# Rows of the activation buffers: A from 512 to 528 elements, B from 576 to 560

## The reference

```
# block 1: T = 256 tokens
a = rms_norm(x);  z = a @ w_in                  # 2048 x 5120: q, k, v, u, g
o = diff_attention(q, k, v) | spatial_gate(gelu(u), gelu(g))
h = x + o @ w_out                               # 2048 x 2048
f = rms_norm(h); h += (silu(f @ w1) * (f @ w3)) @ w2       # hidden 5632
h += (p @ pl_w_up) * sigmoid(h @ pl_w_gate);  x = rms_norm(h)
# block 2: T = 16 learned tokens + 256
hn = rms_norm(h); proj = hn @ w_in_2            # 2048 x 12288
y = g_a * pooled(u) @ pool_w * scale + g_b * ((gb * conv3(gc * v)) @ conv_out_w)
h += y @ w_o;  h += (silu(.) * .) @ w_down      # hidden 5632
out = rms_norm(h)[:, 16:]
```

## Time and profile before

| | |
|---|---|
| time, median of 3 runs | 2670.52 us (2670.02 to 2670.8) |
| span of the profiled execution | 2668.2 us |
| that execution's own time beside its span | not listed; the median is 2.3 us longer than the span |
| TensorE matmul busy | 2657.2 us, 15711 matmuls |
| TensorE weight load busy | 2349.5 us |
| VectorE busy | 1658.2 us |
| ScalarE busy | 1235.8 us |
| HBM read | 498.37 MB, 188 GB/s over the span |

### The profile page before, as it was taken

How to read it: one execution, slowest core, us unless ns; L and a number is a source line. 1 busy time by engine, 2 the same in 40 slices (tenths; PEclk the granted TensorE clock), 3 DMA queues, 4 the chain that set the end, 5 groups by cost and what they waited for, 6 DMA issues and landing times.

```text
span 2668.2 us, 39872 instructions
## 1 busy us (share of the span) xinstructions
PE 2657.2 (100%) x15711; PEld 2349.5 (88%) x15711; DVE 1658.2 (62%) x1645; ACT 1235.8 (46%) x1355; POOL 0.8 (0%) x7
## 2 busy tenths in 40 slices
PE   9999999999999999999999999999999999999998
PEld 7889888888888888888999999888888888888887
DVE  6567766555655556796676666556765645564555
ACT  5446554444444444565443333444554434443444
POOL 0000000000000000000000000000000000000000
PEclk9999999999999999999999999999999999999999
DMA  8554555556555555555555555555565555555554
GB/s 291 183 174 144 192 187 189 191 189 191 192 191 191 191 191 188 175 197 198 176 183 178 179 184 190 189 189 189 189 205 189 189 190 189 189 195 195 178 190 140
DMA packets 254251, 502.92 MB, mean 188 GB/s; under 512 B 8130, under 2 KB 11652, under 8 KB 253988
## 3 DMA queue, kind: packets, MB, share of 16 engines
q1 hardware_dynamic: 252180, 497.61, 56.5%
q10 hardware_dynamic: 1952, 3.68, 0.4%
HBM read 498.37 MB, written 2.88 MB: 188 GB/s over the span
## 4 chain that ended last, share of the span: by engine, by line
PE 99%; DVE 0%; ACT 0%; DMA 0%; issue 0%; ACTq 0%; DVEq 0%
PE ps L1356 49%; PE ps L1370 24%; PE ps L1389 4%; PE ps L1390 4%; PE ps L1391 4%; PE ps L1407 4%; PE ps L1408 4%; PE ps L1409 4%; PE ps L1399 0%; PE ps L1401 0%; PE ps L1400 0%; PE ps L1319 0%; DMA xtok<-in_x_dram 0%; PE ps L1543 0%; PE ps L1542 0%; PE ps L1544 0%
## 5 line engine op out<-in xcount | busy, mean ns | idle before, releaser
L822 DVE TENSOR_TENSOR lo<-raw,hi 128x1024 fp32r<-128x1024 f32 x940 | 1127.6, 1223 | 856.5 <-ACT hi L488 847.6
L488 ACT ACTIVATE hi<-raw 128x1024 fp32r<-128x1024 f32 x940 | 971.3, 1055 | 1065.3 <-PE ps L1370 479.0
L1356 PE MATMUL ps<-A,hi 128*128 128x512 f32 x3648 | 859.9, 392 | 0.0
L1356 PEld LDWEIGHTS ps<-A,hi 128*128 128x128 f32 x3648 | 675.1, 188 | 138.9
L1356 PE MATMUL ps<-B,hi 128*128 128x512 f32 x1984 | 481.7, 395 | 0.0
L1370 PEld LDWEIGHTS ps<-A,lo 128*128 128x128 f32 x3648 | 442.6, 188 | 11.5 <-DVE lo L822 0.2
L1370 PE MATMUL ps<-A,lo 128*128 128x256 f32 x3648 | 445.4, 278 | 0.0
L1356 PEld LDWEIGHTS ps<-B,hi 128*128 128x128 f32 x1984 | 364.4, 188 | 79.3
L1370 PEld LDWEIGHTS ps<-B,lo 128*128 128x128 f32 x1984 | 243.0, 188 | 10.3
L1370 PE MATMUL ps<-B,lo 128*128 128x256 f32 x1984 | 244.5, 277 | 0.0
L1408 PE MATMUL ps<-B,hi 128*128 128x258 f32 (+1 forms) x768 | 219.8, 286 | 0.0
(11 more groups left out here) (240 smaller groups left out, 1341.1 us busy)
## 6 DMA issues: line engine op xcount, KB each, us to landing
raw<-in_w_in_dram SPq DMA_DIRECT2D x136, 1024.0 KB, 5.1
raw<-in_ffn_w_dram SPq DMA_DIRECT2D x132, 1024.0 KB, 5.1
raw<-in_w_gate_up_dram SPq DMA_DIRECT2D x88, 1024.0 KB, 5.0
raw<-in_w_down_dram SPq DMA_DIRECT2D x44, 1024.0 KB, 5.1
raw<-in_w_out_dram SPq DMA_DIRECT2D x16, 1024.0 KB, 5.1
raw<-in_pl_w_gate_dram SPq DMA_DIRECT2D x16, 1024.0 KB, 5.1
raw<-in_conv_out_w_dram SPq DMA_DIRECT2D x16, 1024.0 KB, 5.1
raw<-in_w_o_dram SPq DMA_DIRECT2D x16, 1024.0 KB, 5.1
```

The source lines that it names most:

```text
L488: act.activation(hi[:, slot % RING], raw[:, raw_slot, 2 * (slot % 2):2 * (slot % 2) + 2, :], ACT.Copy).then_inc(hi_ready, 1)
L822: dve.tensor_tensor(lo[:, slot % RING], raw[:, slot // 2 % RAWS, 2 * (slot % 2):2 * (slot % 2) + 2, :], hi[:, slot % RING], ALU.subtract). ...
L1356: last = pe.matmul(ps[:, b0 + m, :], high(slot, kk, m), both, start=j == 0 and kk == 0, stop=ends and j == seg.pieces - 1 and kk == 1)
```

## The change

Rows of A are 528 elements long (2112 bytes) in place of 512 (2048), and those of B 560 (2240) in place of 576 (2304). Nothing is written to or read from the added elements. No instruction, loop or wait is touched; only the addresses are.

```
-BROW = 576
+BROW = 560
+AROW = 528
...
-        A = sb("A", [P, KT, 2 * T], F32R)
+        A = sb("A", [P, KT, AROW], F32R)
```

## The result

The changed kernel takes 2690.91 us (median of 4 runs, 2690.61 to 2691.1) against 2670.44 us before: +20.5 us, ratio 1.0077 with a 95% interval of [1.0065, 1.0089]. It is slower, by 0.8%.

A forecast was written before the change was run, and what follows sets the result against it. TensorE's start-to-start matmul pace was taken to bound the kernel, set by operand distance; terms of +7.8, -4.3, 0, +3.3, +2.3, -0.8 and 0 us gave +8.3, so 2678.8 us, with a range of 2650 to 2697.

The forecast's parts named there:

- rival (c): All rows: new distances as dear as 192 (2693 us), or each change of distance costs a step (+15 us); chance 0.16.
- the forecast's own span: Whole kernel: 2672 to 2686 us if a mix of distances sets the pace; chance 0.36.
- Distance with a period of 256: Moving operand's start less stationary's, modulo 256, sets the pace: 64 cheap, about 228.8 ns; 192 dear, about 233.2.
- The unknown distances: Half the rows, at distances 0 and 128: taken at the mean of cheap and dear, 231 ns for 512 columns.
- high on A: 3648 matmuls of high weights on A: 228.8 to 230.95 ns, +7.8 us.
- low on A: 3648 matmuls of low weights on A: left at 115.45 ns, 0 us.
- low on B: 1984 matmuls of low weights on B: 113.8 to 115.45 ns, +3.3 us.
- the sum of the ends: All terms with the unknown half of the rows at its bounds: -96 us (2574) to +65 us (2735).
- The mix of distances: Rows of A and B taking four distances: each kind's pace is the mean of its parts, no cost of changing.
- by token, B stationary: 1056 matmuls in the segments by token with B stationary: 228.9 to 231.1 ns, +2.3 us.
- A stationary: 384 matmuls in the segments by token with A stationary: 233.3 to 231.1 ns, -0.8 us.
- Wide: 2304 matmuls of 272 and 258 columns on B: 0 us, with bounds of -16 to +11 us.

The follow-up runs named there:

- e1: Kernel before, with vec2 (384 bytes) moved ahead of B so that B has A's distance of 64 from the weights: 2668.2 us, ratio 0.9992.
- e4: Kernel before, with small tensors reordered so that A starts 192 bytes past the weights as B_halves does: 2674.73 us, ratio 1.0017.
- e5: Kernel before, with only the weights (raw, hi, lo) moved by 64 bytes, A and B keeping their addresses: 2686.9 us, ratio 1.0063.
- e7: Kernel before, with only B's rows changed, to 544 elements, so they take distances 192 and 64 in turn: 2673.29 us, ratio 1.0012.
- e11: e9 with segments plgate, ga, gbr, cout and wo added to SNAKED, giving blocks of 32 there: 2671.01 us, ratio 1.0002 against the kernel before.
- e3: Kernel before, with small tensors reordered so that all rows of A and B_halves start 128 bytes past the weights: 2703.66 us, ratio 1.0125.
- e12: Kernel before at its own addresses, with segments plgate, ga, gbr, cout and wo added to SNAKED: 2681.53 us, ratio 1.0044.
- e9: Kernel before, rows unchanged, with A and B_halves 64 bytes past hi and lo 128 bytes further than hi: 2666.71 us, ratio 0.9987.
- e8: Kernel before, rows unchanged, with A and B_halves at distance 0 from hi and lo 64 bytes further than hi: 2669.55 us, ratio 0.9998.
- e2: Kernel before, with small tensors reordered so that A and B_halves both start 0 bytes past the weights: 2676.61 us, ratio 1.0024.

## Why the prediction was right, and where its sum was short

**Direction and range.** Slower, and 2690.9 lies within 2650 to 2697. It lies there because the range had been drawn out to rival (c); the forecast's own span, 2672 to 2686, misses it. The sum took +8.3 us where +20.5 came. The time is nearer to (c)'s 2693, to which I gave 0.16, and (c)'s two mechanisms, dear new distances and a cost of changing, are in part what happened. The direction was no luck: it came from high weights on A, the largest group, leaving a cheap distance, and that term held.

**What bounds the kernel.** Right. No engine and no DMA took part; the +20.8 us of span are steps from matmul to matmul. The strides for VectorE cost nothing (1226 ns for four rows of B before and after).

**Distance with a period of 256.** Right, and shown: e1 and e4 exchange the paces of A and B, and e5 moves them by moving the weights. The period shows after the change as well. In plgate and cout, rows k = 0 to 3 of A take 229.4, 233.8, 233.2 and 230.6 ns for high weights, and rows 4 to 7 take 229.6, 234.2, 233.3 and 230.6, 256 bytes further within 512 (means from the start times). What the prediction didn't have is that distance isn't all: the order and length of the blocks, and the order of the rows, choose among several paces of one distance (e7 to e11). The rule of the Trainium skill ("SBUF — State Buffer", section "Who interferes with whom": two independent read ports, and TensorE never waits on anyone) would have left the time at 2670.5. Measurements decide against it as a statement of pace: 64 bytes on the weights alone cost 16.7 us in e5. Where in the chip the steps are lost no run shows.

**The unknown distances, taken at the mean of the known.** For high weights that was nearly right: 227.8 at 0 and 233.0 at 128, mean 230.4, against my 231. The term "high on A" was +7.8 us and came out at +8.7. For low weights it was wrong: 119.7 and 118.6, against my 115.45. That is the term "low on A: I leave it there, 0" (came out +5.3) and "low on B, +3.3" (+8.0). I had the bound for them at 122.5, and no reason for the middle but that the paces seen were close to one another. The 115.45 wasn't even the middle of what had been seen: it is A's mean, and with B's 113.8 for distance 192 the same rule gives 114.6, that is -3.0 and +1.6 us in place of 0 and +3.3, and a sum further off. (In the sum of the ends, low on B is -5 and +10 us by the values given, not -7 and +11.)

**The mix of distances.** The forecast held that a mix costs the mean of its parts; I had put the cost of changing into (c), as 4.7 ns at each change, +15 us. From the steady table and the changed kernel: on A 231.4 - 230.8 = 0.6 ns a high matmul (+2.3 us) and 117.4 - 117.0 = 0.4 a low one (+1.5); on B 1.4 (+2.8) and 1.0 (+2.1); by token, B stationary, 232.2 against a mean of 230.4 (226.7, 233.3, 232.7 and 228.9 with B at 0, 64, 128 and 192), +1.8 ns (+1.8 us). Together some 10 to 11 us, half of the result, or about 3.2 ns for each of the 3248 changes. e7 shows such an excess by itself, with two distances. That it is paid for each change isn't shown: for low weights it can as well be the dearer of the paces that one distance allows, since with 117.8 for distance 64 the mean of the four is 117.4, what the changed kernel has on A. I dismissed a cost of changing because B's rows jumped by 256 bytes without a trace; that is no jump in distance at all, by the period that I had chosen myself.

**Token and wide segments.** By token, B stationary: +2.3 forecast, +3.3 measured for the 1008; the mean of the four steady paces would have made it +1.5. A stationary -0.8, measured -0.7. Wide 0, measured -2.4 us, within its bounds. (Of the 258-column ones, those of lines 1407 and 1409 start 56 bytes into the row, at 184 modulo 256 and not at 128.)

**What the profile after was to show.** One pace for A and B between 229 and 233: so it is, 231.4 and 232.2. A change of pace with every row: so it is, in the steps of plgate and cout above. B's stages shorter: no. Their high blocks are, by 0.9 ns, but their low ones are longer by 4.0.

## What to carry to other kernels

When TensorE alone bounds a kernel, read start-to-start steps by buffer before anything else: like matmuls on two buffers that differ by nanoseconds can tell of addresses and not of work, and swapping 64 to 384 bytes of small tensors in the allocation is a cheap test of it. Keep the distance between the moving and the stationary operand constant over rows; here a mix of four distances cost some 10 us for their mean being dearer than the paces before, and about as much again above that mean. A distance that is best for one kind of matmul isn't best in sequence with another, so the pace has to be measured in the order in which the blocks will run.

## What the runs showed of the hardware beyond what was expected

- With the weights stationary, the step of a 512-column matmul lies between 227.8 and 233.2 ns and that of a 256-column one between 113.6 and 119.7 (means on A), as the moving operand starts 0, 64, 128 or 192 bytes past the stationary one, modulo 256. All are at a granted clock of 1.00, which is 2.4 GHz, and all lie above the 213.3 and 106.7 ns of the columns. 64 bytes of shift of both buffers are worth up to 1.25% of a kernel (e3).
- At a granted clock of 0.50, which is 1.2 GHz, the steps are the columns alone: 213 to 214 and 426 to 427 ns (e11, e12).
- The pace has more than one steady state at one distance. At 64, low blocks of 32 take 113.1 and 117.8 ns by turns (before, e1), and high blocks 229.1 or 233.1 (e9); at 192 low blocks take 113.4 (e4, e9) or 117.8 (e8). What picks the state is open: e8 to e12 show that it goes with the distance of the blocks between them and with order and length of the blocks, not how.
- It is reproducible: e5 repeats the means of e2 (on A) and e3 (on B) for high and low weights within 0.1 ns on other addresses.
